# A new order of weight slabs in the input projection of a hybrid encoder block, with later summing and attention steps moved to match

## The chip, the cores and the metric

The kernel runs on one core of one Trainium2 chip. The metric is the device time of one execution in microseconds (us). The kernel before takes 1123.92 us, the median of three runs (1123.84 to 1124.09). About 0.2% (2.2 us) is what a measurement of this kernel can tell from no change.

## What is computed

```python
for layer in range(DEPTH):                      # DEPTH = 1, SEQ = 256, D_MODEL = 2048
    h = rms_norm(x, norm1_g[layer])
    proj = h @ w_in[layer]                      # 2048 x 7168
    rq, rk, rv, rg, aq, ak, av = jnp.split(proj, split_at, axis=-1)
    rq, rk = rotary(rq), rotary(rk)             # 8 retention heads of 128
    ret = head_group_norm(retention(rq, rk, rv), ret_norm_g[layer])
    ret = silu(rg) * ret
    aq, ak = rms_norm(aq, q_norm_g), rms_norm(ak, k_norm_g)   # 8 attention heads of 128
    att = chunk_attention(aq, ak, av, rel_bias[layer])        # softmax(scores + bias) @ v
    x = x + jnp.concatenate([ret, att], axis=-1) @ w_out[layer]
    h = rms_norm(x, norm2_g[layer])
    x = x + jnp.square(jax.nn.relu(h @ w_ff1[layer])) @ w_ff2[layer]
```

## The kernel before, in words

All weights are float32 in memory, and each matrix product runs as three products of float32 parts that TensorE takes: the high part of the weights (`w_hi`) with the high and the low part of the activations, and the low part of the weights (`w_lo`) with the high part. ScalarE makes `w_hi` by a copy from the landed slab `raw` (L993), VectorE makes `w_lo` by a subtraction (L1403), so each piece of weights passes ScalarE, then VectorE, then TensorE.

The first third of the kernel is the input projection with attention and retention. It goes in four **head pairs** (BLOCKS = 4); a pair makes attention heads 2i and 2i+1 and retention heads of the same numbers. A pair is a list of 19 **slabs** (STEPS), each of four 128-row tiles of weights, and each slab is worked in two **pieces**, so that a pair has 38 pieces, numbered 0 to 37. The kinds of slab:

- I0 to I3: the four slabs of the first attention head (384 columns, 12 matrix products of a piece). J0 to J3: the second attention head.
- Q1, P5, P6, P7, P3, Q2, P4: the seven **products** of a Strassen-like scheme for the retention columns (512 columns, 6 matrix products of a piece). Some take a sum of slabs as weights (slab `a` plus slab `b`, then plus slab `d`), made by VectorE in place (`in_sum`, L1412), and some take a slab to which a DMA from the GpSimd queue adds (`add_ret`, L543). They take sums of blocks of the normalised x as activations (`sf_hi`, `sf_lo`, the x forms, made once in the first pair, the **lead-in**, from `s_blk`, L1431, and `s_mix`, L1445).
- Z1, Z2, H1, H2: plain slabs for the retention columns that the products leave (512 columns, 12 matrix products of a piece).

Weight slabs land in five slots of `raw`; the order of the loads is the list LOADS, and a slab's slot is free again when VectorE has subtracted its last reader. For piece q + 2 ScalarE makes `w_hi` (`in_hi`) and VectorE `w_lo` (`in_lo`) at position q of their programs; both work in a ring of four, so `w_hi` of piece q waits until TensorE has done piece q - 4.

Between the pieces stand the small steps of the heads. Each engine has a hand-written table (`at_piece(i, position, step)`) that says behind which piece a step comes, and each engine runs its program strictly in that order. For an attention head the chain is: ScalarE reads the finished projection (`att_proj`, tile `a_proj`, L1013) and squares it (`att_squares`, `junk`, L1025); VectorE adds epsilon (`att_mean_squares`, `a_ms`, L1479); GpSimd takes the power (`att_power`, `a_rs`, L534); VectorE scales q and k (`att_norm`, `a_qk`, L1486); TensorE transposes (`att_T`, L624 and L626); ScalarE and VectorE copy (`att_qT`, `att_kT`); TensorE makes the scores (`att_scores`, L632 and L633); VectorE adds the bias and takes the maximum (`att_bias_max`, `a_s`, L1499); ScalarE the exponential (`att_exp`, `a_e`, L1035); VectorE the probabilities (`att_probs`, `a_p`, L1512); TensorE transposes them (`att_PT`, L639) and multiplies by v (`att_pv`, L644). A retention head has `ret_rotate` and `ret_rotated` (`r_qk`, L1538) on VectorE in front of its transposes (`ret_T`, L652), then scores, product with v, group norm, and a last transpose (`ret_ZT`, L676) that `ret_mix` reads on ScalarE (`zT_hi`, L1069) and VectorE (`zT_lo`, L1580).

The products' results move between accumulation banks. `set_z` (VectorE, L1419) writes P5 - P6 into bank Z and must come before P7, which goes on adding into the bank that `set_z` reads. `set_w` (L1425), `set_y` (L1089) and `set_h` (L1094) start the banks W, Y and H. Here a wait of P7 on `set_z` stands in the program of TensorE:

```python
elif step == "P7":
    pe.wait_ge(sf_lo_ok, 3)
    pe.wait_ge(z_set, i + 1)
elif step == "Z1" and m == 1:
    pe.wait_ge(w_set, i + 1)
```

The other two thirds, the output projection and the feed-forward layers, have their own order (SLAB_ORDER) and are not touched.

Of the kernel before, what the change touches and what calls it, by code (L numbers as in the profile page):

```python
# [47 lines left out]
STEPS = "I0 I1 I2 I3 J0 Q1 J1 P5 J2 P6 J3 P7 P3 Z1 Q2 Z2 P4 H1 H2".split()  # L48
LOADS = "I0 I1 I2 I3 J0 a J1 b J2 d J3 Z1 e Z2 H1 H2".split()
# [25 lines left out]
def hybrid_block(nc, x, x_cols, w_att, w_ret, w_out, w_up, w_down, gains, rel_windows, rope_cos, rope_sin, decay, out):  # L75
# [3 lines left out]
    with ExitStack() as ctx:  # L79
# [341 lines left out]
        def _(sp):  # L421
# [55 lines left out]
            for name in LOADS[9:]:  # L477
                load_in(0, name)
# [39 lines left out]
        def _(pool):  # L518
# [62 lines left out]
        def _(pe):  # L581
# [188 lines left out]
            for i in range(BLOCKS):  # L770
                for h, places in ((2 * i, (13, 15, 19, 21)), (2 * i + 1, (27, 28, 31, 33))):
                    for pos, f in zip(places, (att_T, att_scores, att_PT, att_pv)):
                        at_piece(i, pos, f, h)
# [4 lines left out]
                late = i == BLOCKS - 1
                at_piece(i + 1, 1 if late else 3, ret_T, 2 * i + 1)
                at_piece(i + 1, 2 if late else 4, ret_scores, 2 * i + 1)  # L780
                at_piece(i + 1, 3 if late else 5, ret_y, 2 * i + 1)
                at_piece(i + 1, 5 if late else 7, ret_ZT, 2 * i + 1)
# [182 lines left out]
        def _(act):  # L965
# [176 lines left out]
            for i in range(BLOCKS):  # L1142
                h, u, late = 2 * i, 2 * i, i == BLOCKS - 1
                at_piece(i, 8, att_proj, h)
                at_piece(i, 9, att_squares, h)
                at_piece(i, 12, keep_in_q1, i)
                at_piece(i, 13, att_qT, h)
                at_piece(i, 16, keep_in_p5, i)
                at_piece(i, 17, att_exp, h)
                at_piece(i, 19, att_pT, h)  # L1150
                at_piece(i, 21, att_mix, h)
                at_piece(i, 22, att_proj, h + 1)
                at_piece(i, 23, set_y, i)
                at_piece(i, 24, att_squares, h + 1)
                at_piece(i, 25, set_h, i)
                at_piece(i, 27, att_qT, h + 1)
                at_piece(i, 29, att_exp, h + 1)
                at_piece(i, 31, att_pT, h + 1)
                at_piece(i, 32, ret_proj, u)
                at_piece(i, 33, att_mix, h + 1)  # L1160
                at_piece(i, 34, ret_exp, u)
                at_piece(i, 35, ret_qT, u)
# [5 lines left out]
                at_piece(i + 1, 4 if late else 6, ret_scale, u + 1)  # L1168
                at_piece(i + 1, 5 if late else 7, ret_mix, u + 1)
# [227 lines left out]
        def _(dve):  # L1397
# [37 lines left out]
            def s_first():  # L1435
                dve.wait_ge(xc_hi, PIECES)
                dve.wait_ge(xc_lo, PIECES)
                for b in (1, 3, 0, 2):
                    s_block(b)
                dve.wait_ge(s_blk_ok, 4)  # L1440
# [188 lines left out]
            at_piece(0, 17, s_lo, 3)
            for i in range(BLOCKS):  # L1630
                h, u, late = 2 * i, 2 * i, i == BLOCKS - 1
                at_piece(i, 10, att_mean_squares, h)
                at_piece(i, 11, att_norm, h)
                at_piece(i, 11, in_sum, i, "b", "Q1")
                at_piece(i, 13, att_kT, h)
                at_piece(i, 14, in_sum, i, "d", "P5")
# [17 lines left out]
                at_piece(i + 1, 0 if late else 1, ret_rotate, u + 1)  # L1654
                at_piece(i + 1, 0 if late else 2, ret_rotated, u + 1)
# [5 lines left out]
                at_piece(i + 1, 5 if late else 7, ret_mix, u + 1)  # L1661
# [301 lines left out]
```

## Time and profile before

| what | value |
|---|---|
| median of three runs | 1123.92 us |
| the profiled execution's own time | 1123.88 us |
| its span, first to last instruction | 1122.1 us |
| mean granted TensorE clock | 0.998 |
| TensorE (matrix products) busy | 1104.2 us, 98% |
| VectorE busy | 884.6 us, 79% |
| ScalarE busy | 688.3 us, 61% |
| GpSimd busy | 54.2 us, 5% |
| moved by DMA | 263.81 MB, mean 235 GB/s |
| a `w_att` slab (768 KB), from issue to landing | 4.2 us, median of 28 |
| an adding DMA from the GpSimd queue (1,024 KB of `w_ret`) | 8.5 us, median of 8 |

Busy time of TensorE is nearly the whole span, and the places where it stands still are found in the timeline. A row of a timeline gives the start, the length, the engine, the line, the operation, the tile written and those read, the shape and the count, and in square brackets the idle time in front and what ended it. Lengths on TensorE overlap with the next row, so costs are read from start to start.

### The profile page before, as it was taken

Reading aid. Unit: us, or ns where it says so; the run is one execution under the profiler, and the core shown is the slowest. Engines: PE = TensorE matmul, PEld = TensorE weight load, DVE = VectorE, ACT = ScalarE, POOL = GpSimd, SP = SyncE. Lnnn points to the kernel's source line nnn. Section 1 sums busy time; section 2 is a strip of 40 time slices with the busy share of each in tenths; the row PEclk is TensorE's granted clock in tenths of the full one; section 3 lists DMA queues with packets and bytes.
Section 4 is the critical chain, followed back from the end, with each engine's and each line's share of the span. In section 5 each row is a group of like instructions: output and inputs, shape, how many; then the busy total and the mean of one; then the engine's idle time right before and its main releaser. Section 6 shows DMA issues by size and latency. Waiting matters only on the chain.

```text
span 1122.1 us, 13185 instructions
## 1 busy us (share of the span) xinstructions
PE 1104.2 (98%) x5198; PEld 933.7 (83%) x5198; DVE 884.6 (79%) x881; ACT 688.3 (61%) x809; POOL 54.2 (5%) x66
## 2 busy tenths in 40 slices
PE   9799999999999999999999999999999999999998
PEld 9688888988988888888888888888888888888887
DVE  6878777777787768878788778788779788779784
ACT  6565565574565446668756568655667755577652
POOL 0100100100100000000000000000000000000000
PEclk9999999999999999999999999999999999999999
DMA  9785584585576556796797797797787797787792
GB/s 363 261 248 182 156 271 161 166 264 174 169 241 262 187 225 188 230 294 218 233 284 241 249 275 228 230 292 230 262 263 229 247 273 236 257 280 218 246 276 95
DMA packets 42958, 263.81 MB, mean 235 GB/s; under 512 B 4752, under 2 KB 6544, under 8 KB 15120
## 3 DMA queue, kind: packets, MB, share of 16 engines
q1 hardware_dynamic: 36704, 220.22, 52.6%
q0 software_dynamic: 5760, 41.95, 20.3%
q8 instruction: 41, 0.67, 0.2%
q10 hardware_dynamic: 432, 0.81, 0.2%
q14 instruction: 21, 0.17, 0.0%
HBM read 260.85 MB, written 2.10 MB: 234 GB/s over the span
## 4 chain that ended last, share of the span: by engine, by line
PE 85%; DVE 7%; ACT 3%; issue 2%; POOL 1%; ACTq 0%; DVEq 0%
PE acc L869 10%; PE acc L867 10%; PE acc L871 10%; PE acc L739 5%; PE acc L746 5%; PE acc L752 5%; PE bankC L829 4%; PE bankC L824 4%; PE acc L824 4%; PE acc L822 4%; PE bankC L822 4%; PE acc L829 4%; DVE w_lo L1403 3%; PE acc L591 2%; PE acc L596 2%
## 5 line engine op out<-in xcount | busy, mean ns | idle before, releaser
L1690 DVE TENSOR_TENSOR w_lo<-raw,w_hi 128x2048 fp32r<-128x2048 f32 x180 | 410.9, 2288 | 126.9 <-ACT w_hi L1206 126.7
L1206 ACT ACTIVATE w_hi<-raw 128x2048 fp32r<-128x2048 f32 x180 | 344.7, 1916 | 219.5 <-PE acc L871 145.5
L1403 DVE TENSOR_TENSOR w_lo<-raw,w_hi 128x1024 fp32r<-128x1024 f32 (+1 forms) x152 | 167.5, 1106 | 52.4 <-ACT w_hi L993 52.3
L993 ACT ACTIVATE w_hi<-raw 128x1024 fp32r<-128x1024 f32 (+1 forms) x152 | 143.1, 963 | 40.9 <-DVE raw L1412 32.5
L739 PE MATMUL acc<-w_hi,hT_hi 128*128 128x384 f32 (+1 forms) x416 | 105.5, 372 | 0.3 <-ACT w_hi L993 0.2
L867 PE MATMUL acc<-w_hi,hF_hi 128*128 128x512 f32 x256 | 100.8, 394 | 0.0
L871 PE MATMUL acc<-w_hi,hF_lo 128*128 128x512 f32 x256 | 99.7, 390 | 0.0
L869 PE MATMUL acc<-w_lo,hF_hi 128*128 128x512 f32 x256 | 99.7, 389 | 0.0
L746 PE MATMUL acc<-w_hi,hT_lo 128*128 128x384 f32 (+1 forms) x416 | 99.2, 356 | 0.0
L752 PE MATMUL acc<-w_lo,hT_hi 128*128 128x384 f32 (+1 forms) x416 | 98.9, 356 | 0.0
L867 PE MATMUL acc<-w_hi,dF_hi 128*128 128x512 f32 x248 | 96.9, 391 | 0.0
L871 PE MATMUL acc<-w_hi,dF_lo 128*128 128x512 f32 x248 | 96.5, 389 | 0.0
L869 PE MATMUL acc<-w_lo,dF_hi 128*128 128x512 f32 x248 | 96.5, 389 | 0.0
L746 PEld LDWEIGHTS acc<-w_hi,hT_lo 128*128 128x128 f32 x416 | 75.6, 188 | 7.0
L752 PEld LDWEIGHTS acc<-w_lo,hT_hi 128*128 128x128 f32 x416 | 75.4, 188 | 6.5
L739 PEld LDWEIGHTS acc<-w_hi,hT_hi 128*128 128x128 f32 x416 | 72.8, 188 | 6.5 <-ACT w_hi L993 1.0
L1698 DVE TENSOR_TENSOR raw<-raw 128x2048 f32<-128x2048 f32 x32 | 73.1, 2285 | 0.0
L871 PEld LDWEIGHTS acc<-w_hi,hF_lo 128*128 128x128 f32 x256 | 48.0, 188 | 10.1
L867 PEld LDWEIGHTS acc<-w_hi,hF_hi 128*128 128x128 f32 x256 | 48.1, 188 | 9.9
L869 PEld LDWEIGHTS acc<-w_lo,hF_hi 128*128 128x128 f32 x256 | 48.1, 188 | 9.4
L871 PEld LDWEIGHTS acc<-w_hi,dF_lo 128*128 128x128 f32 x248 | 46.6, 188 | 9.7
L867 PEld LDWEIGHTS acc<-w_hi,dF_hi 128*128 128x128 f32 x248 | 46.6, 188 | 9.6
(262 smaller groups left out, 1813.8 us busy)
## 6 DMA issues: line engine op xcount, KB each, us to landing
raw<-in_w_up SPq DMA_DIRECT2D x64, 1024.0 KB, 6.2
raw<-in_w_down SPq DMA_DIRECT2D x64, 1024.0 KB, 6.1
raw<-in_w_ret SPq DMA_DIRECT2D x32, 1024.0 KB, 5.3
raw<-in_w_att SPq DMA_DIRECT2D x28, 768.0 KB, 4.2
raw<-in_w_out SPq DMA_DIRECT2D x16, 1024.0 KB, 4.9
raw<-in_w_up POOLq DMA_DIRECT2D x16, 1024.0 KB, 8.9
raw<-in_w_down POOLq DMA_DIRECT2D x16, 1024.0 KB, 8.6
raw<-in_w_ret POOLq DMA_DIRECT2D x8, 1024.0 KB, 8.5
```

What stands on the lines that cost most here:

```text
L739: nc.tensor.matmul(bank[:, 0:wide], stationary(step, m, t)[0], piece(w_hi, q, start, start + wide), start=fresh, stop=False, skip_group_ch ...
L746: nc.tensor.matmul(bank[:, 0:n], stationary(step, m, t)[1], piece(w_hi, q, start, start + n), start=False, stop=False, skip_group_check=True)
L752: mm = nc.tensor.matmul(bank[:, 0:n], stationary(step, m, t)[0], piece(w_lo, q, start, start + n), start=False, stop=t == SLAB_KT - 1, ski ...
L822: nc.tensor.matmul(bank[:], hi[:, form, tile_cols(t)], wh[:, cols], start=first and t == 0, stop=False, skip_group_check=True)
L824: nc.tensor.matmul(bank[:], lo[:, form, tile_cols(t)], wh[:, cols], start=False, stop=False, skip_group_check=True)
L867: nc.tensor.matmul(banks[m][:], hi[:, form + m, tile_cols(t)], wh[:, cols], start=False, stop=False, skip_group_check=True)
L869: nc.tensor.matmul(banks[m][:], hi[:, form + m, tile_cols(t)], wl[:, cols], start=False, stop=False, skip_group_check=True)
L871: mm = nc.tensor.matmul(banks[m][:], lo[:, form + m, tile_cols(t)], wh[:, cols], start=False, stop=t == SLAB_KT - 1, skip_group_check=True)
L993: nc.scalar.activation(piece(w_hi, q, 0, n), raw[:, r, half * n:(half + 1) * n], ACT.Copy).then_inc(hi_done, 1)
L1206: nc.scalar.activation(w_hi[:, ring(s)], raw[:, r, :], ACT.Copy).then_inc(slab_hi, 1)
L1403: nc.vector.tensor_tensor(piece(w_lo, q, 0, n), raw[:, IN_PLAN[i, READ_AT.get(step, step)][0], half * n:(half + 1) * n], piece(w_hi, q, 0, ...
L1690: nc.vector.tensor_tensor(w_lo[:, ring(s)], raw[:, r, :], w_hi[:, ring(s)].bitcast(f32), ALU.subtract).then_inc(slab_lo, 1)
```

## The change

The four head pairs no longer share one order. The first pair keeps its slabs (FIRST_STEPS, FIRST_LOADS) but moves small steps; pairs 2 to 4 get a new list, in which Q1 comes before I3, each product stands between two attention slabs, and Z1 stands in front of J3. On GpSimd the power for the first attention head now comes behind the DMA that adds to slab `b`. In the lead-in the sums of x blocks are made between the first subtractions, in front of the mean squares of x. `set_w` no longer waits for `set_y`, but `set_y` for `set_w`. Numbers in the tables are positions in the pair; `b` is 1 in pairs 2 to 4.

```diff
-STEPS = "I0 I1 I2 I3 J0 Q1 J1 P5 J2 P6 J3 P7 P3 Z1 Q2 Z2 P4 H1 H2".split()
-LOADS = "I0 I1 I2 I3 J0 a J1 b J2 d J3 Z1 e Z2 H1 H2".split()
+FIRST_STEPS = "I0 I1 I2 I3 J0 Q1 J1 P5 J2 P6 J3 P7 P3 Z1 Q2 Z2 P4 H1 H2".split()
+FIRST_LOADS = "I0 I1 I2 I3 J0 a J1 b J2 d J3 Z1 e Z2 H1 H2".split()
+STEPS = "I0 I1 I2 Q1 I3 J0 P5 J1 P6 J2 P7 P3 Z1 J3 Z2 Q2 P4 H1 H2".split()
+LOADS = "I0 I1 I2 a b I3 J0 d J1 J2 Z1 J3 Z2 e H1 H2".split()
...
@@ GpSimd
-                att_power(2 * i)
                 pool.wait_ge(in_summed, 2 * i + 1)
                 add_ret(i, "b", 1, 1, in_b, i)
+                att_power(2 * i)
...
@@ TensorE
-                for h, places in ((2 * i, (13, 15, 19, 21)), (2 * i + 1, (27, 28, 31, 33))):
+                first = (13, 15, 20, 22), (27, 28, 31, 33)
+                rest = (14, 16, 20, 22), (31, 32, 35, 36)
+                for h, places in zip((2 * i, 2 * i + 1), rest if i else first):
...
-                at_piece(i + 1, 5 if late else 7, ret_ZT, 2 * i + 1)
+                at_piece(i + 1, 5 if late else 8, ret_ZT, 2 * i + 1)
...
@@ ScalarE
             def set_y(i):
-                act.wait_ge(piece_used, in_first(i, "P7") + 2)
+                act.wait_ge(w_set, i + 1)
...
-                at_piece(i, 8, att_proj, h)
-                at_piece(i, 9, att_squares, h)
+                at_piece(i, (8, 10)[b], att_proj, h)
+                at_piece(i, (9, 11)[b], att_squares, h)
...
@@ VectorE
             def set_w(i):
-                dve.wait_ge(y_set, i + 1)
+                dve.wait_ge(piece_used, in_first(i, "P7") + 2)
...
-            at_piece(0, PIECES - 1, x_mean_squares)
-            at_piece(0, PIECES - 1, s_first)
-            at_piece(0, 8, s_second)
+            for pos, b in ((3, 1), (4, 3), (5, 0), (6, 2)):
+                at_piece(0, pos, s_first, b)
+            at_piece(0, PIECES - 1, s_second)
+            at_piece(0, PIECES - 1, x_mean_squares)
...
-                at_piece(i, 10, att_mean_squares, h)
-                at_piece(i, 11, att_norm, h)
-                at_piece(i, 11, in_sum, i, "b", "Q1")
+                at_piece(i, (10, 8)[b], in_sum, i, "b", "Q1")
+                at_piece(i, (14, 12)[b], in_sum, i, "d", "P5")
+                at_piece(i, (10, 12)[b], att_mean_squares, h)
+                at_piece(i, (11, 13)[b], att_norm, h)
...
-                at_piece(i, 14, in_sum, i, "d", "P5")
-                at_piece(i, 20, set_z, i)
+                at_piece(i, (20, 19)[b], set_z, i)
-                at_piece(i, 23, set_w, i)
+                at_piece(i, (24, 22)[b], set_w, i)
...
-                at_piece(i + 1, 0 if late else 1, ret_rotate, u + 1)
-                at_piece(i + 1, 0 if late else 2, ret_rotated, u + 1)
+                at_piece(i + 1, 0, ret_rotate, u + 1)
+                at_piece(i + 1, 0 if late else 1, ret_rotated, u + 1)
```

VectorE in pairs 2 to 4, from the last read of the retention head before (`zT_lo`) to the scaling of the first attention head (`a_qk`). Before:

```order
L1580 SCALAR_TENSOR_TENSOR zT_lo<-bankA,gv,zT_hi 128x256
L1403 TENSOR_TENSOR w_lo<-raw,w_hi 128x1024 x2
L1403 TENSOR_TENSOR w_lo<-raw,w_hi 128x768
L1479 TENSOR_SCALAR a_ms<-a_ss 128x4
L1403 TENSOR_TENSOR w_lo<-raw,w_hi 128x768
L1486 TENSOR_SCALAR a_qk<-a_proj,a_rs 128x128 x4
L1412 TENSOR_TENSOR raw<-raw 128x2048
```

Now:

```order
L1602 SCALAR_TENSOR_TENSOR zT_lo<-bankA,gv,zT_hi 128x256
L1435 TENSOR_TENSOR raw<-raw 128x2048
L1426 TENSOR_TENSOR w_lo<-raw,w_hi 128x768
L1426 TENSOR_TENSOR w_lo<-raw,w_hi 128x1024 x2
L1426 TENSOR_TENSOR w_lo<-raw,w_hi 128x768
L1435 TENSOR_TENSOR raw<-raw 128x2048
L1501 TENSOR_SCALAR a_ms<-a_ss 128x4
L1426 TENSOR_TENSOR w_lo<-raw,w_hi 128x768
L1508 TENSOR_SCALAR a_qk<-a_proj,a_rs 128x128 x4
```

Both sums into slab `a` (`raw<-raw`) now stand between `zT_lo` and the epsilon step `a_ms`; before, the first of them came behind `a_qk` and the second later.

TensorE in pairs 2 to 4, from the first head's scores (bankA) to the product that goes on in bankC. Before (J2 and the first piece of P6; the second piece of P6, `att_PT`, J3 and `att_pv` follow, and then P7):

```order
L632 MATMUL bankA<-a_kT,a_qT 128x128
L633 MATMUL bankA<-a_kT,a_qT 128x256
L739 MATMUL acc<-w_hi,hT_hi 128x384 x4
L746 MATMUL acc<-w_hi,hT_lo 128x384 x4
L752 MATMUL acc<-w_lo,hT_hi 128x384 x4
L739 MATMUL acc<-w_hi,hT_hi 128x384 x4
L746 MATMUL acc<-w_hi,hT_lo 128x384 x4
L752 MATMUL acc<-w_lo,hT_hi 128x384 x4
L739 MATMUL bankC<-w_hi,sf_hi 128x512 x2
L746 MATMUL bankC<-w_hi,sf_lo 128x512 x2
L752 MATMUL bankC<-w_lo,sf_hi 128x512 x2
```

Now (the second piece of P6, J2, and the first rows of P7):

```order
L637 MATMUL bankA<-a_kT,a_qT 128x128
L638 MATMUL bankA<-a_kT,a_qT 128x256
L744 MATMUL bankC<-w_hi,sf_hi 128x512 x2
L751 MATMUL bankC<-w_hi,sf_lo 128x512 x2
L757 MATMUL bankC<-w_lo,sf_hi 128x512 x2
L744 MATMUL acc<-w_hi,hT_hi 128x384 x4
L751 MATMUL acc<-w_hi,hT_lo 128x384 x4
L757 MATMUL acc<-w_lo,hT_hi 128x384 x4
L744 MATMUL acc<-w_hi,hT_hi 128x384 x4
L751 MATMUL acc<-w_hi,hT_lo 128x384 x4
L757 MATMUL acc<-w_lo,hT_hi 128x384 x4
L744 MATMUL bankC<-w_hi,sf_hi 128x512 x2
```

P7 must wait for `set_z`, which on VectorE stands behind the probabilities of this head. Between the scores and P7 there were two attention slabs and P6; now there are one piece of P6 and one attention slab.

## Rows read from the trace of the kernel before

**Rows 1.** TensorE's waits: engine line <- releaser: us in total, times, longest.

```profile
PE bankD L739 <- ACT w_hi L993: 4.4, 4, 2.6
PE bankB L639 <- DVE a_p L1512: 3.0, 4, 1.4
```

**Rows 2.** TensorE's timeline, pair 2 and the start of pair 3.

```profile
98.23 1.06 PE L739 MATMUL acc<-w_hi,hT_hi 128*128 128x512 f32 x4
...
117.92 0.38 PE L676 MATMUL bankA<-ident,r_zn 128*128 128x128 f32 x2
...
122.45 0.63 PE L739 MATMUL bankC<-w_hi,hT_hi 128*128 128x512 f32 x2
...
125.21 0.87 PE L739 MATMUL acc<-w_hi,hT_hi 128*128 128x384 f32 x4
...
127.32 0.85 PE L739 MATMUL acc<-w_hi,hT_hi 128*128 128x384 f32 x4
...
147.91 0.71 PE L739 MATMUL bankC<-w_hi,sf_hi 128*128 128x512 f32 x2
...
180.65 0.59 PE L661 MATMUL bankC<-r_qT,r_kT 128*128 128x256 f32 x2
...
184.63 1.06 PE L739 MATMUL acc<-w_hi,hT_hi 128*128 128x512 f32 x4
```

**Rows 3.** ScalarE's timeline, pair 2.

```profile
119.66 1.04 ACT L1013 ACTIVATE a_proj<-acc,rstd 128x384 f32<-128x384 f32 x2
...
121.53 0.31 ACT L1025 ACTIVATE junk<-a_proj 128x128 f32<-128x128 f32 x1
...
122.70 1.57 ACT L993 ACTIVATE w_hi<-raw 128x768 fp32r<-128x768 f32 x2
...
129.48 1.06 ACT L993 ACTIVATE w_hi<-raw 128x1024 fp32r<-128x1024 f32 x1 [5.20 <-DVE raw L1412]
```

**Rows 4.** VectorE's timeline, pair 2.

```profile
118.84 0.48 DVE L1580 SCALAR_TENSOR_TENSOR zT_lo<-bankA,gv,zT_hi 128x256 fp32r<-128x256 f32 x1 [0.24 <-ACT zT_hi L1069]
...
127.16 2.29 DVE L1412 TENSOR_TENSOR raw<-raw 128x2048 f32<-128x2048 f32 x1
...
130.57 1.22 DVE L1403 TENSOR_TENSOR w_lo<-raw,w_hi 128x1024 fp32r<-128x1024 f32 x1 [1.12 <-ACT w_hi L993]
...
142.65 0.95 DVE L1403 TENSOR_TENSOR w_lo<-raw,w_hi 128x768 fp32r<-128x768 f32 x1
...
162.15 0.28 DVE L1499 TENSOR_TENSOR a_s<-bankA,bias 128x128 f32<-128x128 f32 x1
...
181.56 0.56 DVE L1553 TENSOR_TENSOR r_sT<-bankC,dec 128x384 f32<-128x384 f32 x1 [0.20 <-PE bankC L662]
```

**Rows 5.** GpSimd's power, lead-in and pair 2.

```profile
35.57 1.65 POOL L534 TENSOR_TENSOR a_rs<-a_ms,neg_half 128x4 f32<-128x4 f32 x1 [0.46 <-DVE a_ms L1479]
...
154.57 1.03 POOL L534 TENSOR_TENSOR a_rs<-a_ms,neg_half 128x4 f32<-128x4 f32 x1 [12.20 <-DVE a_ms L1479]
```

**Rows 6.** ScalarE's exponential of the second head, pair 2.

```profile
163.65 0.40 ACT L1035 ACTIVATE a_e<-a_s,a_nmx 128x128 f32<-128x128 f32 x1 [1.73 <-DVE a_nmx L1505]
```

**Rows 7.** TensorE's timeline, the lead-in (also VectorE's scaling step).

```profile
37.26 0.88 DVE L1486 TENSOR_SCALAR a_qk<-a_proj,a_rs 128x128 f32<-128x128 f32 x4 [0.91 <-POOL a_rs L534]
...
38.19 0.44 PE L624 MATMUL bankA<-ident,a_qk 128*128 128x128 f32 x2
...
41.48 1.22 PE L739 MATMUL bankD<-w_hi,sf_hi 128*128 128x512 f32 x2 [2.63 <-ACT w_hi L993]
...
46.17 0.46 PE L632 MATMUL bankA<-a_kT,a_qT 128*128 128x128 f32 x2
...
61.51 0.71 PE L739 MATMUL bankC<-w_hi,sf_hi 128*128 128x512 f32 x2
```

**Rows 8.** Busy time by window: us, engines (x count), granted clock, DMA.

```profile
38.00:41.00 3.00, 0.85 (x6) 0.42 (x5) 2.33 (x2) 0.63 (x1) 0.34 (x1) 1.00 0.92 381
41.00:45.00 4.00, 3.52 (x9) 2.81 (x10) 3.54 (x5) 3.48 (x6) 0.71 (x1) 0.57 0.72 122
```

More of the change, by code:

```diff
@@ L349, in hybrid_block, with steps @@
         PLAN = raw_plan()
+        def steps(i):
+            return STEPS if i else FIRST_STEPS
         def in_slab(i, step):
-            return len(STEPS) * i + STEPS.index(step)
+            return len(STEPS) * i + steps(i).index(step)
         def in_first(i, step):
@@ L360, in in_plan @@
             for i in range(BLOCKS):
-                for name in LOADS:
+                for name in LOADS if i else FIRST_LOADS:
                     r = min(free, key=lambda r: free[r])
@@ L374, in in_step @@
             i, n = divmod(s, len(STEPS))
-            return i, STEPS[n], half
+            return i, steps(i)[n], half
         def in_cols(step):
@@ L476, in _ @@
             load_decay(1)
-            for name in LOADS[9:]:
+            for name in FIRST_LOADS[9:]:
                 load_in(0, name)
@@ L1154, in _ @@
[L1154 to L1162, printed above, removed]
+                b = int(i > 0)
+                if b:
+                    at_piece(i, 8, keep_in_q1, i)
@@ new lines, in _ @@
+                at_piece(i, (8, 10)[b], att_proj, h)
+                at_piece(i, (9, 11)[b], att_squares, h)
+                if not b:
+                    at_piece(i, 12, keep_in_q1, i)
+                at_piece(i, (16, 14)[b], keep_in_p5, i)
+                at_piece(i, (13, 14)[b], att_qT, h)
+                at_piece(i, 17, att_exp, h)
+                at_piece(i, 20, att_pT, h)
+                at_piece(i, 22, att_mix, h)
+                at_piece(i, (22, 28)[b], att_proj, h + 1)
+                if b:
+                    at_piece(i, 28, set_h, i)
+                    at_piece(i, 29, att_squares, h + 1)
+                    at_piece(i, 30, set_y, i)
+                    at_piece(i, 31, att_qT, h + 1)
+                    at_piece(i, 32, ret_proj, u)
+                    at_piece(i, 33, att_exp, h + 1)
+                    at_piece(i, 34, ret_exp, u)
+                    at_piece(i, 35, att_pT, h + 1)
+                    at_piece(i, 35, ret_qT, u)
+                    at_piece(i, 36, att_mix, h + 1)
+                else:
+                    at_piece(i, 24, set_y, i)
+                    at_piece(i, 24, att_squares, h + 1)
+                    at_piece(i, 25, set_h, i)
+                    at_piece(i, 27, att_qT, h + 1)
+                    at_piece(i, 29, att_exp, h + 1)
+                    at_piece(i, 31, att_pT, h + 1)
+                    at_piece(i, 32, ret_proj, u)
+                    at_piece(i, 33, att_mix, h + 1)
+                    at_piece(i, 34, ret_exp, u)
+                    at_piece(i, 35, ret_qT, u)
@@ L1167, in _ @@
                 at_piece(i + 1, 1 if late else 3, ret_qT, u + 1)
-                at_piece(i + 1, 4 if late else 6, ret_scale, u + 1)
-                at_piece(i + 1, 5 if late else 7, ret_mix, u + 1)
+                at_piece(i + 1, 4 if late else 7, ret_scale, u + 1)
+                at_piece(i + 1, 5 if late else 8, ret_mix, u + 1)
             for q in range(8 * G_OUT):
@@ L1433, in s_block, with s_first @@
                                         hT_lo[:, tiles, tile_cols(m)].bitcast(f32), ALU.add).then_inc(s_blk_ok, 1)
[L1435 to L1440, printed above, removed]
+            def s_first(b):
+                dve.wait_ge(xc_hi, SLAB_KT)
+                dve.wait_ge(xc_lo, SLAB_KT)
+                s_block(b)
             def s_mix_of(f, a, b, op, after):
@@ L1452, in s_second @@
             def s_second():
+                dve.wait_ge(s_blk_ok, 4)
                 s_mix_of(0, s_blk[:, 1, :], s_blk[:, 3, :], ALU.subtract, 0)
@@ L1660, in _ @@
                 at_piece(i + 1, 3 if late else 5, ret_norm, u + 1)
-                at_piece(i + 1, 5 if late else 7, ret_mix, u + 1)
+                at_piece(i + 1, 5 if late else 8, ret_mix, u + 1)
             for q in range(8 * G_OUT):
```

38 lines of the change are left out of this document (15 added, 23 removed).

## The prediction, made before the result was known

> **What bounds the kernel now.** I read the busy shares first: TensorE is busy for 98% of the span, and the change adds or removes no matrix product, so only the moments at which TensorE stands still, or runs slowly, can change. The list of TensorE's waits comes next [rows 1]; the reader should see that they are few and all in the head pairs: a product's `w_hi` (4.4 us, the longest 2.6) and the probabilities (3.0, the longest 1.4). Then TensorE's timeline of one pair [rows 2]: pair 2 runs from 98.23 to 184.63, so a pair takes **86.4**; pairs 3 and 4 repeat it. Last come the timelines of ScalarE, VectorE and GpSimd [rows 3 to 5], whose step lengths are all that a new order needs. Costs are taken from start to start.
>
> **The change, in pairs 2 to 4.** The same work is reordered, so I walk one pair with the lengths of before, time zero at its start. TensorE: an attention piece 2.11, the two pieces of a product 2.76 together [rows 2]. A `w_lo` occupies VectorE for 0.87 or 1.14 (its length less the 0.08 by which the next row overlaps) [rows 4].
>
> 1. *Start.* `ret_rotate` and `ret_rotated` move up by a position. r_qk is then ready before TensorE asks, and the wait in front of the second retention head's transposes goes: -0.7 (an estimate from its idle time, below the longest wait of [rows 1]). The transpose `ret_ZT` came at 117.92 - 98.23 = 19.7 [rows 2]; now one attention piece less (-2.1), one product more (+2.76) and that wait less lie in front: **19.6**.
>
> 2. *First attention head up to its transposes.* VectorE is in order, and from `zT_lo` to `a_qk` it now has both sums. The chain behind `ret_ZT`: `zT_lo` starts 0.92 later (117.92 to 118.84) [rows 2, 4]; +0.40 to the first sum; +2.32 to the `w_hi` of P5 (127.16 to 129.48) [rows 3, 4]; +0.95 to `a_proj`; +1.87 over `a_proj` and a `w_hi` to the squares (119.66 to 121.53); +1.17 to the next `w_hi` (to 122.70) [rows 3]; +0.87 to its `w_lo`, +0.87 to the second sum, +2.21 to `a_ms` (2.29 less overlap) [rows 4]; +0.24 to the power; +1.69 to `a_qk` (35.57 to 37.26) [rows 5, 7]; +0.93 to the transposes (37.26 to 38.19) [rows 7]. Sum 14.4: transposes at **34.0**. TensorE's own way there is I3's second piece, J0, P5 and J1's first piece: 4 x 2.11 + 2.76 + 0.2 for small steps = 11.4, so it arrives at 31.0. **New wait: 3.0.** Before, P5's wait stood near here (4.4 in four waits with the lead-in's 2.6, so 0.6 a pair) [rows 1]; it goes, because the first sum is now three positions ahead of it.
> The power is 1.65 long when a `w_lo` runs beside it and 1.03 when VectorE is idle at its start [rows 5]. Here `w_lo` of piece 15 is ready and follows `a_ms` at once, so I take 1.65; with 1.03 the wait would be 2.4.
> The Trainium skill (SBUF - State Buffer, "SBUF: two separate sides") says that GpSimd and VectorE share a pair of ports under an exclusive lock, which a VectorE operation with two inputs in SBUF holds for its whole length. By that rule too the longer power is the right one here, and the wait is 3.0; were it left aside, 2.4.
>
> 3. *From the scores to P7.* Scores come at 34.0 + 0.4 (transposes) + 2.11 + 1.38 = 37.9. Behind them: bias +0.91 (180.65 to 181.56, a step of the same shape) [rows 2, 4]; exponential +1.50 (162.15 to 163.65) [rows 4, 6]; its two parts 0.9; `w_hi` of P7 to its `w_lo` +1.09 (129.48 to 130.57); that `w_lo` 1.14; probabilities 0.66 (an estimate from two VectorE steps of 128 to 256 columns); another `w_lo` 1.14; `set_z` 0.74. Sum 8.1, P7 at **46.0**. TensorE's own way is P6's second piece, J2 and the scores: 1.4 + 4.2 + 0.5 = 6.1. **New wait: 1.9.** Before, a whole J slab more lay in between, and `set_z` never held P7.
>
> 4. *The rest.* Before, P7 to the end took 184.63 - 147.91 = 36.7 [rows 2]. J3 (4.2) and the product with v (0.6) are moved behind P7: 41.5. The second head has slack: by the same steps `a_qk` is ready 1.5 ahead of its transposes, the scores' copies 0.8 ahead; only r_qk comes 0.3 late, since VectorE has the second head's probabilities and the rotation together. Pair: 46.0 + 41.5 + 0.3 = **87.8, against 86.4: +1.4**, three times +4.2. The waits removed come to 3.4 a pair; 4.9 to 5.2 come in.
>
> 5. *Transfers.* Of the slots, J1's has the shortest time: its slot is freed at position 7 and read at 12. In the walk that is 18.5 to 27.2, nearly 9 us; a slab of `w_att` landed in 4.2 us in the median (table above). Nothing late. The addition into slab `b` is issued at 24 and read past 41. On GpSimd the power stands behind this DMA, but the DMA's sum is done 8 us before `a_ms`. Cost 0.
>
> **The lead-in.** Before, TensorE waited 2.63 for P5, and the granted clock then fell to 0.57 on average over four us [rows 8]; P5 took 41.48 to 46.17 [rows 7], 4.7 in place of 2.76. Now the four block sums (0.61 each) fill VectorE's idle time between 16 and 24, and slab `b` is summed before the epsilon step. But the mean squares of x, hence `rstd` and `a_proj`, come 1.8 later, and the power waits for the DMA's issue (about 1.0). The walk gives transposes at 40.6 in place of 38.19, P5 at 40.9 at full clock, done at 44.0 in place of 46.17; a new wait of 1.3 for P6's `w_lo`; the 1.4 in front of `att_PT` gone. P7 starts at 57.4, and with the product with v moved behind it that is **-3.5** against 61.51. Then `set_w` and, behind it, `set_y` come later than before: waits of 0.8 (Z1's second bank), 0.4 (a `w_hi`) and 0.8 (transposes), **+2.0**. Together -1.5.
>
> **The clock.** What a wait of 3.0 does to the clock in pairs 2 to 4 no row shows directly. The nearest: idle 2.63, the clock fell and 1.9 was lost [rows 7, 8]; idle 1.4, no slow stretch behind it [rows 1]. The bounds are 0 and 1.9 for each of three pairs, 0 and +5.7. 3.0 lies nearest the row that fell; yet that one came behind a stretch with several short waits, which pairs 2 to 4 lack. I take less than half of it, +1.4 in all, and keep both ends.
>
> **The sum**, against the profiled execution's own 1123.88 (the median is 1123.92, the same): +4.2 - 1.5 + 1.4 = +4.1, so **1128.0**.
>
> **Rivals.**
> - *A, the forecast*: both new waits stand. From 1126 (no fall of the clock) to 1132 (three falls). For it: each step has its row. Against: fifteen steps in a row, each taken without slack. Chance 0.50.
> - *B, both waits, but shorter*: `w_hi` copies and sums start a little sooner, the power at 1.03, no fall: 0.6 to 1.0 less a pair. 1123.9 - 1.5 + 3 x 0.6 = 1124.2. Chance 0.22.
> - *C, the wait at the first head's transposes doesn't come (faster)*. Place: VectorE between `zT_lo` and `a_ms`. It decides by whether ScalarE delivers J1's `w_hi` by about 24 rather than 27.2, so that the second sum runs while TensorE is in P5. Then only P7's wait of 1.9 is left, a pair is 84.8, and the kernel 1123.9 - 4.8 - 1.5 = 1117.6; with P7's wait gone too, 1112. For it: VectorE has 2 us idle in the walk there. Against: the first sum is held by `zT_lo`, and ScalarE by the first sum. Chance 0.22.
> - *D, transfers late*: the order of loads has less slack for J1 and J2 (5 and 7 positions in place of 9); one late slab of 1 to 3 us a pair: 1133. The adding DMAs landed in 8.5 us (table above). Chance 0.04.
> - *E, the lead-in's gain is lost*, its clock falling again: +2. Chance 0.02 by itself; it widens the others.
>
> **How the numbers follow.** About 0.2% (2.2 us) is what a measurement tells from no change: faster is below 1121.7, slower above 1126.1. A gives slower 0.43, the same 0.07; B the same 0.17, faster 0.03, slower 0.02; C faster 0.20, the same 0.02; D and E slower 0.06. Sum: faster 0.23, same 0.26, slower 0.51. The range 1117 to 1132 takes in A, B and C with one wait, and leaves out C with none, D, and A with more than three losses, about 0.15. Forecast A's own range is 1126 to 1132.
>
> **What would show it.** In pairs 2 to 4: an idle time of TensorE near 3 at the transposes of the first head, ended by `a_qk`; near 1.9 before P7, ended by `set_z` (bank Z on VectorE); none before the second retention head's transposes; pair length 87.8 (more where the granted clock falls). In the lead-in: P5 without a 2.6 idle and at full clock, P7 near 57.4, a short wait at Z1's second bank. Wrong would be: a pair under 86.4; `a_ms` ending before 28 in the pair; or a DMA named as the releaser of a `w_hi`.

## The result, and the profile after

The changed kernel takes **1135.27 us** in the median of four runs (1132.64 to 1137.88), against 1123.99 before: ratio 1.010, 95% interval 1.007 to 1.0131. It is slower, as forecast, but by 11.3 us in place of 4.1, and outside the range (1117 to 1132). The runs lie far apart: 1132.64 and 1133.12, then 1137.42 and 1137.88. The profiled execution is one of the first two: 1133.12 us, 9.24 more than the profiled execution before.

TensorE's waits, for [rows 1] (engine line <- releaser: us in total, times, longest):

```profile
PE bankA L629 <- DVE a_qk L1508: 10.4, 5, 2.8
PE bankC L744 <- DVE acc L1442: 5.4, 3, 1.8
PE bankC L744 <- ACT w_hi L1000: 2.2, 2, 1.9
...
PE bankA L657 <- DVE r_qk L1560: 0.9, 1, 0.9
PE acc L744 <- DVE acc L1448: 0.5, 1, 0.5
```

The two forecast waits lead the list: the first attention head's transposes wait for `a_qk` (2.82 in each of pairs 2 to 4; the other two are in the lead-in), and P7 waits for `set_z` (L1442), three times 1.8. Once each, TensorE waits 1.9 for a `w_hi` and 0.5 for `set_w`, both in the lead-in. The wait on `r_qk` is left only behind pair 4, at 373.50.

Busy time by window, pairs 2, 3 and 4 (stretch and its length, then PE, PEld, DVE, ACT, POOL busy with their counts, the granted clock, the DMA share, GB/s):

```profile
98.50:186.81 88.31, 83.69 (x437) 74.70 (x436) 67.27 (x112) 50.32 (x90) 5.92 (x6) 1.00 0.62 195
186.81:276.77 89.96, 85.33 (x437) 75.96 (x436) 67.27 (x112) 50.33 (x90) 5.93 (x6) 0.98 0.61 192
276.77:366.67 89.90, 85.30 (x438) 76.31 (x436) 67.90 (x112) 51.02 (x90) 5.93 (x6) 0.98 0.64 206
```

These rows hold nearly the whole result. A pair took 86.4 before; now it takes 88.31, of which TensorE is idle for 4.62 (88.31 - 83.69), which is 2.82 + 1.80. In pairs 3 and 4 the idle time is the same (4.63 and 4.60), but TensorE's work itself takes 1.6 longer, and the granted clock is 0.98 in place of 1.00: the same matrix products ran partly at the lower of the two levels, 1.2 in place of 2.4 GHz. The same view of short windows finds where: behind P7's wait in pair 3, behind the transposes' wait in pair 4, and in the lead-in at P5.

```profile
232.00:237.00 5.00, 3.96 (x12) 3.24 (x13) 2.02 (x3) 0.48 (x2) 0.00 (x0) 0.66 0.94 333
234.00:235.00 1.00, 1.00 (x4) 0.81 (x3) 0.02 (x1) 0.00 (x0) 0.00 (x0) 0.50 0.69 199
310.50:315.50 5.00, 4.65 (x19) 4.57 (x20) 3.92 (x6) 2.50 (x4) 0.91 (x1) 0.66 0.60 236
41.00:46.00 5.00, 4.02 (x13) 3.36 (x14) 4.95 (x10) 3.08 (x6) 0.02 (x1) 0.66 0.99 241
```

Inside such a window the clock is 0.50, half of full; a mean of 0.66 over 5 us is then 3.4 us at half and 1.6 at full. I call this a **slow stretch**; the one of pair 3 costs 1.65 (89.96 - 88.31).

TensorE's timeline, pair 2, for [rows 2]: `ret_ZT`, the transposes, P7.

```profile
118.09 0.38 PE L681 MATMUL bankA<-ident,r_zn 128*128 128x128 f32 x2
...
132.56 0.44 PE L629 MATMUL bankA<-ident,a_qk 128*128 128x128 f32 x2 [2.82 <-DVE a_qk L1508]
...
144.71 0.70 PE L744 MATMUL bankC<-w_hi,sf_hi 128*128 128x512 f32 x2 [1.80 <-DVE acc L1442]
```

VectorE's timeline, pair 2, for [rows 4]: second sum (L1435), epsilon step, a `w_lo`, scaling; under it GpSimd's power, for [rows 5].

```profile
126.61 0.96 DVE L1426 TENSOR_TENSOR w_lo<-raw,w_hi 128x768 fp32r<-128x768 f32 x1 [0.67 <-ACT w_hi L1000]
127.48 2.28 DVE L1435 TENSOR_TENSOR raw<-raw 128x2048 f32<-128x2048 f32 x1
129.69 0.16 DVE L1501 TENSOR_SCALAR a_ms<-a_ss 128x4 f32<-128x4 f32 x1
129.76 0.95 DVE L1426 TENSOR_TENSOR w_lo<-raw,w_hi 128x768 fp32r<-128x768 f32 x1
131.64 0.87 DVE L1508 TENSOR_SCALAR a_qk<-a_proj,a_rs 128x128 f32<-128x128 f32 x4 [0.93 <-POOL a_rs L539]
...
129.94 1.66 POOL L539 TENSOR_TENSOR a_rs<-a_ms,neg_half 128x4 f32<-128x4 f32 x1 [7.02 <-DVE a_ms L1501]
```

`a_ms` had its input long before: ScalarE's squares ended at 125.8. It stood behind the sum.

The lead-in, for [rows 7]. Before, the last step of the mean squares, the first power (`rstd`) and `a_proj`:

```profile
26.75 0.17 DVE L1614 TENSOR_SCALAR me<-ms 128x2 f32<-128x2 f32 x1
27.07 1.02 POOL L527 TENSOR_TENSOR rstd<-me,neg_half 128x2 f32<-128x2 f32 x1 [25.57 <-DVE me L1614]
28.67 1.04 ACT L1013 ACTIVATE a_proj<-acc,rstd 128x384 f32<-128x384 f32 x2
```

After, in order of time: the same three, the `w_hi` behind `a_proj`, and TensorE at Q1's second piece; then the power of the first head, the transposes, P5 and P7.

```profile
28.83 0.17 DVE L1636 TENSOR_SCALAR me<-ms 128x2 f32<-128x2 f32 x1
29.09 1.22 DVE L1426 TENSOR_TENSOR w_lo<-raw,w_hi 128x1024 fp32r<-128x1024 f32 x1
...
29.16 1.74 POOL L532 TENSOR_TENSOR rstd<-me,neg_half 128x2 f32<-128x2 f32 x1 [27.65 <-DVE me L1636]
...
30.97 1.05 ACT L1020 ACTIVATE a_proj<-acc,rstd 128x384 f32<-128x384 f32 x2 [1.92 <-POOL rstd L532]
31.92 1.05 ACT L1000 ACTIVATE w_hi<-raw 128x1024 fp32r<-128x1024 f32 x1
...
33.02 0.73 PE L744 MATMUL bankC<-w_hi,hT_hi 128*128 128x512 f32 x2 [1.93 <-ACT w_hi L1000]
...
38.90 1.05 POOL L548 DMA_DIRECT2D raw<-in_w_ret  x1 [3.51 <-DVE raw L1435]
39.65 1.38 POOL L539 TENSOR_TENSOR a_rs<-a_ms,neg_half 128x4 f32<-128x4 f32 x1
...
41.98 0.69 PE L629 MATMUL bankA<-ident,a_qk 128*128 128x128 f32 x2 [1.45 <-DVE a_qk L1508]
...
42.75 1.20 PE L744 MATMUL bankD<-w_hi,sf_hi 128*128 128x512 f32 x2
...
58.93 0.63 PE L744 MATMUL bankC<-w_hi,sf_hi 128*128 128x512 f32 x2
```

Pair 2 starts at 98.50, where it had started at 98.23 (the eight profiled executions with this lead-in lie between 98.36 and 98.82). The account of the profiled execution closes: lead-in +0.27, pairs +1.91, +3.56 and +3.50, together 9.24.

### The profile page after: what moved, and what is told of

It is laid out like the page before. It is cut to its first block, busy times and chain, and to the rows that moved or that the text cites. A ratio compares the mean times of both kernels' runs of the same rounds, so it can differ in the third digit from the quotient of the medians.

```text
span 1131.3 us, 13187 instructions
## 1 busy us (share of the span) xinstructions
PE 1105.0 (98%) x5198; PEld 936.3 (83%) x5198; DVE 885.1 (78%) x881; ACT 691.2 (61%) x809; POOL 54.7 (5%) x66
## 4 chain that ended last, share of the span: by engine, by line
PE 89%; DVE 4%; ACT 2%; issue 1%; POOL 1%; DVEq 0%; ACTq 0%; POOLq 0%
PE acc L874 10%; PE acc L878 10%; PE acc L876 10%; PE acc L744 5%; PE acc L751 5%; PE acc L757 5%; PE bankC L836 4%; PE acc L836 4%; PE acc L829 4%; PE bankC L829 4%; PE bankC L831 4%; PE acc L831 4%; PE acc L596 2%; PE acc L601 2%; PE acc L608 2%
```

## The experiments

Two theories of the pairs: each new wait is a **queue on VectorE**, a step whose input is ready standing behind work that nobody waits for yet (against it: ScalarE's late `a_proj`, or too little work between the steps in the new order of slabs); and the spread between runs is **the clock** behind those waits. For the lead-in: the forecast gain never came, or came and was given back elsewhere. Line numbers differ by a few between the kernels.

**1. The old lead-in under the new pairs.** The changed kernel, with every step of the first pair as before.

```diff
-            for pos, b in ((3, 1), (4, 3), (5, 0), (6, 2)):
-                at_piece(0, pos, s_first, b)
-            at_piece(0, PIECES - 1, s_second)
             at_piece(0, PIECES - 1, x_mean_squares)
+            at_piece(0, PIECES - 1, s_first)
+            at_piece(0, 8, s_second)
...
```

> The changed kernel with the first pair's steps and the GpSimd and set_w/set_y orders of the first pair as in the kernel before; pairs 2 to 4 as changed. Theory (the lead-in is worth nothing, the whole loss is in pairs 2 to 4): pair 2 starts at 98.2, the pairs keep waits of 2.8 and 1.8, and the time stays within 1 us of the changed kernel (1132.9 where two stretches at half clock come, more where more come). Rival (the new lead-in does save the 1.5 of the forecast, and something outside it gave that back): the time rises to 1134.5 or more with the same number of stretches at half clock.

Measured: 1133.71 (1131.2 to 1134.55), ratio 1.0083, interval 1.0068 to 1.0098. In its profiled execution (1131.2) pair 2 starts at 98.25, the waits are 2.8 and 1.8 again, and the pairs take 88.30, 88.32 and 89.93: one slow stretch.

```profile
98.25:186.55 88.30, 83.67 (x438) 74.67 (x436) 67.28 (x112) 50.34 (x90) 5.92 (x6) 1.00 0.62 195
186.55:274.87 88.32, 83.69 (x438) 74.70 (x436) 67.26 (x112) 50.33 (x90) 5.91 (x6) 1.00 0.62 195
274.87:364.80 89.93, 85.31 (x438) 75.87 (x436) 67.89 (x112) 50.98 (x90) 5.91 (x6) 0.98 0.64 206
```

The changed kernel's 1133.12 less one slow stretch (1.65) and less the lead-in's 0.27 is 1131.2 too. So the rival, 1134.5 or more at the same number of slow stretches, falls, and the loss is in pairs 2 to 4. The other three runs (1133.07 to 1134.55) have no trace.

**2. The new lead-in alone**, over the old pairs: the same lines, put into the kernel before.

> The kernel before with the new first pair alone; pairs 2 to 4 in the old order. Theory: pair 2 starts at 98.5 in place of 98.2 and the pairs stay at 86.4, so 1124.2, no measurable change; the power of x's scale takes 1.7 beside a w_lo in place of 1.0, TensorE waits 1.9 at Q1's second piece, and P5 runs at half clock as before. Rival (forecast of the lead-in): 96.7 and 1122.4. Neither waits of 2.8 nor of 1.8 in pairs 2 to 4; the spread between runs stays as small as that of the kernel before (0.3 us), since it comes from stretches at half clock behind those waits.

Measured: 1124.06 over ten runs against 1124.07, interval 0.9991 to 1.0009; pair 2 starts at 98.43, the pairs take 86.42. The forecast's 1122.4 is out. The runs spread over 0.8 us, a little more than expected and far less than the 5 of the changed kernel. TensorE waits 1.92 at Q1's second piece, as expected, but here the slow stretch comes behind this wait, before P5, and P5 runs at full clock:

```profile
34.00:39.00 5.00, 4.79 (x17) 3.78 (x16) 4.41 (x6) 3.03 (x10) 0.54 (x2) 0.66 1.02 376
41.00:46.00 5.00, 4.07 (x22) 3.07 (x21) 4.87 (x9) 3.17 (x6) 0.10 (x1) 1.00 1.00 241
```

Pair 2 starts no earlier for it: the slow stretch is paid in either place.

**3. Scaling first.** In pairs 2 to 4 the epsilon step and the scaling stand ahead of the second sum.

```diff
-                at_piece(i, (14, 12)[b], in_sum, i, "d", "P5")
-                at_piece(i, (10, 12)[b], att_mean_squares, h)
-                at_piece(i, (11, 13)[b], att_norm, h)
+                at_piece(i, (10, 11)[b], att_mean_squares, h)
+                at_piece(i, (11, 12)[b], att_norm, h)
+                at_piece(i, (14, 12)[b], in_sum, i, "d", "P5")
```

> The changed kernel, but in pairs 2 to 4 VectorE has the epsilon step and the scaling of the first head one position earlier, ahead of the second sum into slab a. Theory (the wait of 2.8 at the first head's transposes comes from that sum of 2.2 standing in front of a_ms): a_ms ends 3.8 earlier, the transposes' wait is gone, at most 1.0 comes back at the w_lo of J1's second piece and of P6, which now stand behind the sum; a pair is 1.8 to 2.8 shorter, the kernel 5 to 9 below the changed kernel, and stretches at half clock become fewer. Rival (the wait is set by ScalarE's late a_proj and squares, three positions later than they could be): a_ms stays near where it is, and the wait shrinks by less than 1.

Measured: 1126.94 (1125.3 to 1128.58, six runs), ratio 1.0026, 8 below the changed kernel. VectorE in pair 2, and GpSimd's power:

```profile
126.19 0.17 DVE L1501 TENSOR_SCALAR a_ms<-a_ss 128x4 f32<-128x4 f32 x1
126.92 0.96 DVE L1426 TENSOR_TENSOR w_lo<-raw,w_hi 128x768 fp32r<-128x768 f32 x1 [0.56 <-ACT w_hi L1000]
127.80 0.87 DVE L1508 TENSOR_SCALAR a_qk<-a_proj,a_rs 128x128 f32<-128x128 f32 x4
128.59 2.28 DVE L1435 TENSOR_TENSOR raw<-raw 128x2048 f32<-128x2048 f32 x1
...
126.45 1.03 POOL L539 TENSOR_TENSOR a_rs<-a_ms,neg_half 128x4 f32<-128x4 f32 x1 [3.22 <-DVE a_ms L1501]
```

`a_qk` now starts 29.0 into the pair (127.80 - 98.82) and not 33.1, and TensorE doesn't wait for it in any of the three pairs. The late sum makes no `w_lo` late. But P7's wait has grown:

```profile
PE bankC L744 <- DVE acc L1442: 8.0, 3, 2.7
```

So 2.82 is saved and 0.9 given back at the next queue: the pair is 86.33 without a slow stretch. The rival (ScalarE sets the wait) falls.

**4. `set_z` early**, two positions up, ahead of P7's first `w_lo` and the probabilities.

```diff
-                at_piece(i, (20, 19)[b], set_z, i)
+                at_piece(i, (20, 17)[b], set_z, i)
```

> The changed kernel, but in pairs 2 to 4 set_z stands two positions earlier, ahead of the first w_lo of P7 and of the probabilities. Theory (P7 waits 1.8 because set_z is queued behind two w_lo and the probabilities, though P6 has long been done): P7's wait is gone, the pair is 1.8 shorter, the kernel 5.4 shorter, and more if the stretch at half clock behind it goes too. Rival (P7 would wait for its own w_lo instead, or set_z now waits for P6 on VectorE and holds the probabilities): 0 to 2 in all.

Measured: 1126.68 over ten runs (1124.99 to 1128.07), ratio 1.0023. No wait on `set_z` is left in the list, nothing took its place, and the pairs without a slow stretch take 86.26 and 86.29: 2.05 less than 88.31, 1.8 of it the wait. The median is 8.6 below the changed kernel's, where the wait alone would give 5.4. In the profiled execution (1125.51, 7.6 less) the pairs account for 3 x 2.05 and one slow stretch less for 1.6.

**5. Both repairs together.**

> Both repairs together in pairs 2 to 4 of the changed kernel: epsilon step and scaling ahead of the second sum, and set_z two positions earlier. Theory (the new order of slabs is sound, and its loss is only these two queues on VectorE): both waits are gone, since the 2.7 that P7 still waited with the first repair alone is set_z's; a pair is 86.3 - 2.7 = 83.6, below the 86.4 of before, no stretch at half clock in pairs 2 to 4, and the time 1115.5 to 1116.5, 0.7% below before, with a spread between runs as small as before's. Rival (the new order has no room left, and a w_lo or w_hi comes late in place of each repaired wait): 1121 or more.

Measured: **1114.99** (1114.83 to 1115.37), ratio 0.9922, interval 0.9907 to 0.9937. The three pairs:

```profile
98.36:181.78 83.42, 83.42 (x437) 74.79 (x436) 67.20 (x112) 50.18 (x90) 5.29 (x6) 1.00 0.65 206
181.78:265.20 83.42, 83.42 (x438) 74.82 (x436) 67.22 (x112) 50.19 (x90) 5.29 (x6) 1.00 0.65 207
265.20:348.62 83.42, 83.42 (x438) 74.82 (x436) 67.84 (x112) 50.95 (x90) 5.29 (x6) 1.00 0.68 223
```

Length and busy time of TensorE are equal: it never stands still. The new order of slabs has room for all its work and beats the old order (86.42, of which 84.31 busy) by 3.0 a pair. The time is half a microsecond below the expected band, and the runs lie within 0.6 us again.

**6. No `w_lo` beside the power.** The scaling right behind the epsilon step, so that VectorE waits while GpSimd takes the power; over the changed kernel.

```diff
-                at_piece(i, (11, 13)[b], att_norm, h)
+                at_piece(i, (11, 12)[b], att_norm, h)
```

> The changed kernel, but in pairs 2 to 4 the scaling a_qk stands right behind the epsilon step, so that no w_lo runs on VectorE while GpSimd takes the power. If the w_lo beside it makes the power long (1.65 in place of 1.03), the power is 1.03 here and the wait at the transposes 2.82 - 0.6 = 2.2. If the length has another cause (the tile, the place in the program), it stays 1.65 and the wait 2.8 or, with the a_qk started at once, 2.7.

Measured: 1131.1 (two runs). GpSimd and TensorE in pair 2:

```profile
129.89 1.03 POOL L539 TENSOR_TENSOR a_rs<-a_ms,neg_half 128x4 f32<-128x4 f32 x1 [7.02 <-DVE a_ms L1501]
...
131.89 0.44 PE L629 MATMUL bankA<-ident,a_qk 128*128 128x128 f32 x2 [2.19 <-DVE a_qk L1508]
```

The power is 1.03 and the wait 2.19 (2.82 - 0.63): the `w_lo` beside it did make it long. Three times 0.63 is also what the run is below the changed kernel's 1133.12 with the same two slow stretches.

**7. The lead-in repaired**, over the old pairs as in 2: mean squares ahead of the two `s_mix` sums, and on GpSimd the power ahead of the DMA issue. Against the kernel of 2:

```diff
-                if i:
-                    att_power(2 * i)
+                att_power(2 * i)
                 pool.wait_ge(in_summed, 2 * i + 1)
                 add_ret(i, "b", 1, 1, in_b, i)
-                if not (i):
-                    att_power(2 * i)
...
-            at_piece(0, PIECES - 1, s_second)
             at_piece(0, PIECES - 1, x_mean_squares)
+            at_piece(0, PIECES - 1, s_second)
```

> The kernel before with the new first pair, but the mean squares of x ahead of the two s_mix sums, and on GpSimd the power ahead of the DMA issue. Theory (the lead-in lost its gain to these two): a_proj starts at 29.5 in place of 31.0, TensorE's wait at Q1's second piece falls from 1.9 to 0.5 or less, a_qk comes 1.5 to 2 earlier (the power begins as soon as a_ms is done), pair 2 starts at 96.5 to 97.5 in place of 98.4, and the time is 1 to 2 us below before. Rival (what bounds the stretch is the second sum chain and the clock): pair 2 starts at 98.0 or later, no measurable change.

Measured: 1121.32 over ten runs, ratio 0.9977, interval 0.9968 to 0.9987. Pair 2 starts at 95.70, 2.7 earlier than in 2 and earlier than expected: the first power is 1.01, since `s_mix` runs beside it and no `w_lo`, `a_proj` starts at 28.91, the wait at Q1's second piece is gone, and so is the slow stretch. VectorE's and GpSimd's timelines:

```profile
27.51 0.68 DVE L1449 TENSOR_TENSOR s_mix<-s_blk 128x512 f32<-128x512 f32 x1
...
27.76 1.01 POOL L527 TENSOR_TENSOR rstd<-me,neg_half 128x2 f32<-128x2 f32 x1 [26.26 <-DVE me L1619]
```

The window from the start of J0 in the lead-in to that of pair 2, at a clock of 1.00:

```profile
24.58:95.70 71.12, 67.12 (x321) 54.88 (x321) 58.39 (x94) 44.06 (x81) 6.10 (x6) 1.00 0.78 254
```

**8. Of the two, only the mean squares**, without the lines on GpSimd.

> The kernel before with the new first pair, and of the two repairs of the lead-in only the first: mean squares of x ahead of the two s_mix sums, the power still behind the DMA issue. With both repairs pair 2 started at 95.7, with none at 98.4. Theory (the mean squares carry the most: they cost a_proj 1.5 and the wait that they made was followed by a stretch at half clock of 1.7; the DMA issue holds the power for 1.0): pair 2 at 96.2 to 96.8, 1121.8 to 1122.4. Rival (the order on GpSimd carries the most, through the wait at the first head's transposes): 97.5 or later, 1123.3 or more. The stretch at half clock may come back, since the wait at the transposes is 1.6 here and not 0.8: then 1.7 more on either side.

Measured: 1121.95 over ten runs, ratio 0.9982, interval 0.9972 to 0.9991; pair 2 at 96.37. The mean squares carry 2.06 of the 2.73, the order on GpSimd 0.67. The transposes wait 1.43, and no slow stretch follows, so the 2.06 holds the slow stretch that is gone as well.

**9. The retention head's rotation back** at its old position, over experiment 5.

```diff
-                at_piece(i + 1, 0, ret_rotate, u + 1)
-                at_piece(i + 1, 0 if late else 1, ret_rotated, u + 1)
+                at_piece(i + 1, 0 if late else 1, ret_rotate, u + 1)
+                at_piece(i + 1, 0 if late else 2, ret_rotated, u + 1)
```

> The kernel with both repairs in pairs 2 to 4 (1115.0), but ret_rotate and ret_rotated of the late retention head back at their old positions. Theory (the move upward took away TensorE's wait on r_qk, 0.7 by the forecast, in front of the second retention head's transposes): the wait is back with 0.6 to 0.9 in each of three pairs, and the time rises by 1.8 to 2.7, to 1116.8 to 1117.7. Rival (the wait was taken away by the later position of other steps, or is hidden): within 0.5 of 1115.0.

Measured: 1117.39 (1117.18 to 1117.73), 2.4 more. The wait is back, three times 0.58 beside the 0.9 at the end that all these kernels have, and a pair is 84.20, which is 0.78 more, 0.58 of it the wait.

```profile
PE bankA L657 <- DVE r_qk L1560: 2.6, 4, 0.9
```

**10. All four repairs.**

> All four repairs: the changed kernel with epsilon step and scaling ahead of the second sum, set_z two positions earlier, mean squares of x ahead of the s_mix sums, and in the first pair the power ahead of the DMA issue. The gains lie in different stretches and should add: 1115.0 - (1124.06 - 1121.32) = 1112.3, 1.0% below before. Rival (the lead-in's gain is given back, as pair 2 starts 2.7 earlier against transfers that do not move): 1114 to 1115.

Measured: **1112.34** (1112.31 to 1112.42), ratio 0.9896, interval 0.9881 to 0.9911, the best version: 22.9 below the changed kernel and 11.7 below the one before. The gains add.

**11. The changed kernel again**, for its spread.

> The changed kernel unaltered, again. Its runs had fallen in two groups, near 1132.9 and near 1137.6. Theory (each run has its own number of stretches at half clock of 3.4 us behind the waits of 2.8 and 1.8, each worth 1.6 to 1.7): the times lie on steps about 1.6 apart between 1129 (none in pairs 2 to 4) and 1139 (six), each with the mean granted clock that goes with its number of stretches, and the pairs without one take 88.3, those with one 89.9 to 90.0. Rival (a cause outside the clock, such as transfers): runs of the two groups with the same mean granted clock.

Measured: 1135.16 in the median of four, that is 1132.66 at a mean granted clock of 0.995, 1134.75 at 0.994, 1135.57 and 1135.84 at 0.992. With the first four (0.995 twice, then 0.991 for 1137.42 and 1137.88) the time rises as the clock falls, so the rival, groups with the same mean clock, is out. The expected steps of 1.6 don't show cleanly in these eight times. The profiled execution has two slow stretches in the pairs as well, but elsewhere: at the transposes' waits of pairs 2 and 3, while pair 4 has none.

```profile
98.38:188.22 89.84, 85.23 (x437) 76.29 (x436) 67.25 (x112) 50.37 (x90) 5.92 (x6) 0.98 0.62 192
188.22:277.87 89.65, 85.02 (x438) 76.03 (x436) 67.34 (x112) 50.38 (x90) 5.92 (x6) 0.98 0.61 192
277.87:366.20 88.33, 83.71 (x437) 74.69 (x436) 67.90 (x112) 50.94 (x90) 5.92 (x6) 1.00 0.65 210
```

How many the other runs had is an estimate and not seen: 1137.6 is 4.7 above 1132.9, at 1.65 each three more, so five behind six waits. A pair with two of them stands in no trace.

## Why the prediction was wrong, by its own steps

The sum was +4.1 and the profiled execution showed +9.2. The direction, both waits in the pairs and their places and releasers were right; three terms were too small.

| term | forecast | measured | missed by |
|---|---|---|---|
| pairs 2 to 4 without the clock | 3 x 1.4 = +4.2 | 3 x 1.9 = +5.7 | 1.5 |
| lead-in, slow stretch included | -1.5 | +0.3 | 1.8 |
| the clock in the pairs | +1.4 | +3.2 (two slow stretches); +8 in the slowest run, an estimate | 1.8 and more |

*Step 1, start.* Right: `ret_ZT` at 19.59 (19.6), and the wait on `r_qk` gone. Moving it back cost 0.78 a pair (0.7).

*Step 2, transposes.* Right: at 34.06 (34.0), wait 2.82 (3.0). The power was 1.66 as taken, and experiment 6 shows both its prices. By the Trainium skill (SBUF — State Buffer, "SBUF: two separate sides") whichever of the two operations starts first holds the shared ports for its whole length. For the `w_lo` the traces agree: already running, it makes the power 1.66; starting 0.47 after the power (experiment 3) it leaves it at 1.03. For `s_mix`, which also has two inputs in SBUF and starts 0.25 before the power in experiment 7, they don't: 1.01. In the kernel before it was 1.02 beside `s_blk`, a sum of the same kind. There the measurement decides, and the reason stays open.

*Step 3, P7.* Right: at 46.2 (46.0), wait 1.80 (1.9).

*Step 4, the rest.* It took 42.1 in place of 41.8. This and the 0.2 of step 3 are the 0.5 a pair that the walk fell short. The 0.3 for a late `r_qk` did not come: behind P7's wait TensorE has no wait up to the end of the pair, so its work there is 0.6 more than the 41.5 of the walk. About 0.3 of that (an estimate from starts) is the first head's `att_PT`, which also moved behind P7's first piece and isn't in the walk; the rest is not traced to a step.

```profile
146.17 0.49 PE L644 MATMUL bankB<-ident,a_p 128*128 128x128 f32 x3
```

The other sum of this step, 3.4 of waits removed against 4.9 to 5.2 new, doesn't fit the traces either. A pair before had only 2.1 of idle time (86.40 less 84.26 busy). With 0.6 less of work that makes 2.7 removed, against 4.6 new.

*Step 5, transfers.* Right: no DMA is among the releasers of TensorE's waits, and experiment 5 leaves TensorE no idle time that a late slab could hide in.

*The lead-in* failed, and rival E, with 0.02, was what happened. The step was "the mean squares of x, hence `rstd` and `a_proj`, come 1.8 later". The mean squares came 2.1 later and `a_proj` 2.3 (28.67 to 30.97), since the first power now stood beside a `w_lo` and took 1.74 in place of 1.02, the very case that step 2 priced. I carried the delay to the transposes but not to what is queued behind `a_proj` on ScalarE, the `w_hi` of Q1's second piece: a wait of 1.93 that the prediction doesn't have. The transposes came at 41.98 in place of 40.6, and "P5 at full clock" failed as well: it ran at half clock from 42.75 and ended at 46.83, not at 44.0. In the other profiled execution of this kernel, as in experiment 2, P5 ran at full clock and the slow stretch lay right behind the 1.93, with the same end (pair 2 at 98.38). So what failed is the missing wait of 1.93 with a slow stretch behind it or behind the next wait; experiment 8, which takes this wait away, has none. The forecast wait of 1.3 for P6's `w_lo` came where P5 ran at full clock (0.97 in experiment 2) and not here. P7 stood at 58.93 (57.4), 1.5 late. From there to pair 2 the forecast +2.0 came to +2.25, though the three waits it was made of were shorter: 0.55, 0.18 and 0.50 of idle time.

*The clock.* The mechanism was named, its size wrong twice. I bounded it by three slow stretches, one for each 3.0, and gave P7's wait of 1.9 none. There are six waits, and those of 1.8 brought slow stretches as well. And I took a single number for what differs from run to run: that alone moves this kernel over 5 us. The range's upper end of 1132 was forecast A with three; from the same terms (1126.6 + 6 x 1.9), six would have been 1138.

*Rival C*, no wait at the transposes, was not the changed kernel but is what experiment 3 made: the slack was there (VectorE's idle time in the walk), and the order of the steps didn't use it.

## What to carry to other kernels

When slabs are put in a new order, walk each in-order engine again and ask of every step whether its input is ready before its turn: here two steps, standing behind work that nobody yet waited for, turned a gain of 3.0 a pair into a loss of 1.9, and moving them cost nothing. Carry a delay on to all that is queued behind the late instruction, not only to its own reader. Count TensorE's waits of the lengths seen here (1.8 to 2.8 us) twice, once for their length and once for the slow stretch that may follow, and give the range the case in which it follows every one.

## What the runs showed of the hardware that was not expected

*The same waits bring a slow stretch in one execution and none in another.* The profiled executions with waits of 1.8 to 2.8 in pairs 2 to 4 (the changed kernel twice, experiments 1, 3, 4 and 6) hold 30 such waits and 9 slow stretches, each 3.4 long; a pair has one or none. Eight began 0.1 to 1.3 us after the end of the wait. One, in pair 3 of experiment 11, began 0.6 before it and cost only 1.3 (89.65 - 88.31), the others 1.5 to 1.7. The executions without such waits (experiments 2, 5 and 7 to 10) have none in pairs 2 to 4, also behind waits of 0.6.

In the lead-in it is steadier. All eight executions with the wait of 1.9 at Q1's second piece have exactly one slow stretch there: three behind this wait, five some 9 us later, at the transposes' wait of 1.4. Experiment 8, with a wait of 1.43 at the transposes and without the one of 1.9, has none. What decides about place and number is not shown by any run.

*GpSimd's power.* For an attention head (128x4) it is 1.03 to 1.04 alone, 1.64 to 1.66 where a `w_lo` of 768 columns already runs, and 1.37 to 1.38 right behind the issue of a DMA, whose end it overlaps. For the scale of x (128x2) it is 1.58 to 1.77 where a `w_lo` of 1024 columns already runs, and 1.01 to 1.02 beside `s_mix` or `s_blk`.
